# Block transposes on VectorE in place of TensorE's transposes for the modulation vector of the attention heads

## The reference, cut to what matters

```python
c_act = jax.nn.silu(c)                           # (1, 1024)
for i in range(DEPTH_2):
    mod = c_act @ w_ada[i] + b_ada[i]            # (1, 6 * 1024)
    sh1, sc1, g1, sh2, sc2, g2 = jnp.split(mod, 6, axis=-1)
...
shf, scf = jnp.split(c_act @ w_ada_final + b_ada_final, 2, axis=-1)
```

## Time and profile before

| | |
|---|---|
| median of 3 runs | 1554.79 us (1554.63 to 1555.78) |
| the profiled execution's own time | 1554.12 us |
| its span, first to last instruction | 1552.0 us |
| around the span | 2.12 us |
| instructions | 21277 |
| TensorE busy | 1537.0 us, 99% |
| VectorE / ScalarE / GpSimd busy | 790.5 / 597.4 / 869.6 us |
| mean granted TensorE clock | 0.998 |

### The profile page before, as it was taken

The page is one execution under the profiler, slowest core; times in us unless marked ns, Lnnn a source line. Parts: engine busy times, 40 slices in busy tenths (PEclk is TensorE's granted clock), DMA queues, the critical chain, the costliest instruction groups (busy, mean ns, idle before and its releaser), DMA issues.

```text
span 1552.0 us, 21277 instructions
## 1 busy us (share of the span) xinstructions
PE 1537.0 (99%) x7254; PEld 1273.8 (82%) x7254; DVE 790.5 (51%) x1128; ACT 597.4 (38%) x885; POOL 869.6 (56%) x1040
## 2 busy tenths in 40 slices
PE   9999999999999999999999999999999999999997
PEld 7777878887988888888888888888889888888886
DVE  6887776878645543551545424446257454011113
ACT  7444434685522212223444334244345322122223
POOL 6445538647567765775463635535535766555551
PEclk9999999999999999999999999999999999999999
DMA  6534455226265555542232322313212563223321
GB/s 231 191 128 155 164 214 189 82 84 205 95 216 176 202 198 183 192 160 95 89 114 67 109 82 80 97 52 106 95 54 82 201 206 120 98 95 95 95 82 55
DMA packets 58249, 202.97 MB, mean 131 GB/s; under 512 B 6480, under 2 KB 8528, under 8 KB 58192
## 3 DMA queue, kind: packets, MB, share of 16 engines
q1 hardware_dynamic: 56752, 198.74, 37.6%
q10 hardware_dynamic: 1440, 3.44, 0.7%
HBM read 200.05 MB, written 2.10 MB: 130 GB/s over the span
## 4 chain that ended last, share of the span: by engine, by line
PE 76%; POOL 12%; issue 11%; DVE 0%; DMA 0%; ACT 0%; SPq 0%; POOLq 0%; DVEq 0%; ACTq 0%
PE banks L1708 20%; PE banks L1712 20%; PE banks L1711 20%; POOL w_lo L411 12%; PE banks L2212 2%; PE banks L2211 2%; PE banks L2208 2%; PE banks L1724 1%; PE banks L1727 1%; PE banks L1728 1%; PE banks L2248 1%; PE banks L2247 1%; PE banks L2246 1%; PE banks L2235 0%; PE banks L2234 0%
## 5 line engine op out<-in xcount | busy, mean ns | idle before, releaser
L411 POOL TENSOR_TENSOR w_lo<-w_raw,w_hi 128x256 fp32r<-128x256 f32 x1028 | 862.6, 872 | 646.9 <-ACT w_hi L443 646.9
L443 ACT ACTIVATE w_hi<-w_raw 128x1024 fp32r<-128x1024 f32 x257 | 270.1, 1057 | 640.7 <-PE banks L1708 576.0
L1708 PE MATMUL banks<-a_hi,w_lo 128*128 128x512 f32 x1228 | 483.4, 394 | 0.2 <-POOL w_lo L411 0.2
L1712 PE MATMUL banks<-a_hi,w_hi 128*128 128x512 f32 x1228 | 478.2, 389 | 0.0
L1711 PE MATMUL banks<-a_lo,w_hi 128*128 128x512 f32 x1228 | 478.0, 389 | 0.0
L1708 PEld LDWEIGHTS banks<-a_hi,w_lo 128*128 128x128 f32 x1228 | 230.8, 188 | 49.0 <-issue 1.6
L1712 PEld LDWEIGHTS banks<-a_hi,w_hi 128*128 128x128 f32 x1228 | 230.5, 188 | 48.3
L1711 PEld LDWEIGHTS banks<-a_lo,w_hi 128*128 128x128 f32 x1228 | 230.6, 188 | 47.6 <-issue 1.0
L1708 PE MATMUL banks<-b_hi,w_lo 128*128 128x512 f32 x572 | 224.2, 392 | 2.3 <-POOL w_lo L411 2.1
L1712 PE MATMUL banks<-b_hi,w_hi 128*128 128x512 f32 x572 | 222.6, 389 | 0.0
L1711 PE MATMUL banks<-b_lo,w_hi 128*128 128x512 f32 x572 | 222.6, 389 | 0.0
(11 more groups left out here) (287 smaller groups left out, 1632.7 us busy)
## 6 DMA issues: line engine op xcount, KB each, us to landing
w_raw<-in_W SPq DMA_DIRECT2D x258, 512.0 KB, 3.5
ada_raw<-in_ADA SPq DMA_DIRECT2D x112, 512.0 KB, 4.3
X<-in_XT SPq DMA_DIRECT2D x8, 256.0 KB, 6.4
scr<-in_DECAY ACTq DMA_DIRECT2D x4, 448.0 KB, 4.0
out<-X SPq DMA_DIRECT2D x2, 512.0 KB, 3.0
w_raw<-in_W SPq DMA_DIRECT2D x2, 256.0 KB, 3.8
scr<-in_PT ACTq DMA_DIRECT2D x1, 512.0 KB, 4.8
scr<-in_ROPE ACTq DMA_DIRECT2D x1, 512.0 KB, 4.6
```

The lines of the kernel that those rows point to most:

```text
L411: pool.tensor_tensor(w_lo[:, c % RING, part], w_raw[:, c % RING, part], w_hi[:, c % RING, part].bitcast(fp32), ALU.subtract).then_inc(wlo, 1)
L443: act.activation(w_hi[:, c % RING, :], w_raw[:, c % RING, :], ACT.Copy).then_inc(whi, 1)
L1708: mm = pe.matmul(out, lo, x_hi, start=first, stop=False)
L1712: mm = pe.matmul(out, hi, x_hi, start=False, stop=last)
```

## The change

`ada_turn`, with its eight TensorE transposes a head at n = 17, goes. So does the branch of `ada_out` with two reductions from PSUM. In place of them VectorE transposes `ada_acc` in 32 x 32 blocks into `tmp` and sums it after L1285, TensorE makes four small products at n = 23, and `ada_out` adds the bias from `aux`. The folding matrix is made once ahead of the heads by three additions on VectorE.

```diff
+        head_turned = tmp[:, :, :].rearrange("p a s -> p (a s)")
+        head_fold, head_part = scr[:, 14 * S + 64:14 * S + 96], scr[:, 14 * S + 96:14 * S + 128]
...
-            def ada_out(u, g, at=flat, bank=None):
+            def ada_out(u, g, at=flat):
...
-                if bank is None:
-                    dve.tensor_tensor(dst, aux[:, 0:KD], b, ALU.add).then_inc(aux_free, 1)
-                    return
-                for n, half in enumerate((bank, 7)):
-                    turned = banks[:, half, :].rearrange("p (f q) -> p f q", q=P)
-                    ins = dve.tensor_reduce(ada_col[:, 4 * n:4 * n + 4], turned, AX.X, ALU.add)
-                link(ins, at)
-                dve.tensor_tensor(dst, ada_col, b, ALU.add).then_inc(aux_free, 1)
+                dve.tensor_tensor(dst, aux[:, 0:KD], b, ALU.add).then_inc(aux_free, 1)
...
+            def head_ada_fold(at):
+
+                dve.wait_ge(ada_sum, at("ada", KD))
+                dve.wait_ge(mix_ready, at("two", 2))
+                link(dve.transpose(head_turned, ada_acc[:, :]), at)
+                ins = dve.tensor_reduce(head_part, head_turned.rearrange("p (j q) -> p j q", q=32), AX.X, ALU.add)
+                ins.then_inc(head_folded, 1)
...
             link(dve.memset(G[:, 0:2], 0.0))
+            link(dve.tensor_tensor(head_fold, ident[:, 0:32], ident[:, 32:64], ALU.add))
+            for n in (2, 3):
+                link(dve.tensor_tensor(head_fold, head_fold, ident[:, 32 * n:32 * n + 32], ALU.add))
             dve.wait_ge(r_ready, 1)
...
-                ada_out(A0 + 6, 0, at, 4)
+                head_ada_fold(at)
+                ada_out(A0 + 6, 0, at)
...
-            def ada_turn(at, u, g, bank):
-
-                pe.wait_ge(ada_sum, at("ada", KD * (g + 1)))
+            def head_ada_rows(at, u):
+
+                pe.wait_ge(head_folded, at("one", 1))
                 pe.wait_ge(aux_free, at("aux", u))
-                for f in range(KD):
-                    out = banks[:, bank if f < KD // 2 else 7, f % 4 * P:(f % 4 + 1) * P]
-                    mm = pe.transpose(out, ada_acc[:, f * P:(f + 1) * P], ident)
+                for b in range(4):
+                    mm = pe.matmul(aux[32 * b:32 * b + 32, 0:KD], head_fold, head_part[:, b:32:4], start=True, stop=True)
                 mm.then_inc(aux_ready, 1)
...
-                if n == 17:
-                    ada_turn(at, A0 + 6, 0, 4)
+                if n == 23:
+                    head_ada_rows(at, A0 + 6)
```

More of the change, by code:

```diff
@@ L236, in build @@
         ada_in = [sem(f"ada_in{s}") for s in range(ADA_RING)]
-        ada_sum, ada_folded = sem("ada_sum"), sem("ada_folded")
+        ada_sum, ada_folded, head_folded = sem("ada_sum"), sem("ada_folded"), sem("head_folded")
         x_in = [sem(f"x_in{m}") for m in range(KD)]
```

## The result

The changed kernel takes 1561.3 us, median of 6 runs (1560.6 to 1564.97), against 1555.04 of 6 for the kernel before: ratio 1.0044, 95% interval 1.0033 to 1.0054 (the ratios are as recorded and differ by up to 0.0005 from the quotients of the medians, here 1.0040). It is slower, as forecast, but by 6.3 us, half as much again as the 4.2 that I had, and outside the range (1557.2 to 1560.6). Its profiled execution took 1564.64, with a span of 1562.7 against 1552.0.

A forecast was written before the change was run, and what follows sets the result against it. TensorE, busy 1537.0 of 1552.0 us, was taken to bound the kernel. Three heads lose 1.41, 1.38 and 1.38, in sum 4.17: 1554.12 + 4.17 = 1558.3, and the median 0.67 higher, 1559.0; range 1557.2 to 1560.6.

The forecast's parts named there:

- the mechanism and its sign: Head ends: `ada_out` waits for the small products ahead of two evacuations, which TensorE awaits; three heads slower, 4.17 us.
- the two prices on TensorE: In each head, eight transposes cost 0.88 us and four small products 0.38, so TensorE alone saves 0.50.
- the fourth head: Last head, no next one: its 0.50 us gain goes into a longer wait for `w_lo`, counted 0.
- the clock: Rival: TensorE's clock falls in the new 2.0 us standstills, 9.3 us more, 1568; chance 3%.
- the whole span's mean of 0.998 is a loss of 3.1 us at the start: Whole span: mean clock read as a 3.1 us loss at the start, used to price a fall after each standstill.
- the longest wait now is 1.33 us and the clock is 1.00 after it: TensorE before the change: full clock after its longest wait, 1.33 us, set against a fall in new waits of 2.0.
- the slack of the fold: Before the small products: VectorE's fold is ready 0.1 to 0.3 us early in the first head, 0.4 in the second.
- One small term: Signal from the fold's end on VectorE to TensorE's small products: some 0.05 us.
- a late fold: Rival: block transpose beside GpSimd and ScalarE takes 0.5 us more, TensorE waits, up to 1.5 more, 1560.5; chance 10%.
- whatever it sheds is gained: Inside the heads TensorE never waits, busy in all of 52.6 us, so all work removed from it is saved time.

The follow-up runs named there:

- pad_again: Changed kernel with eight unread 128x512 TensorE products between the small products and the wait for the next head's query and key, run beside the changed kernel: 1559.23 us, 1.0025.
- no_out: Changed kernel without `ada_out` for the heads, so their modulation vectors stay zero and VectorE goes straight from the fold to the evacuations: 1554.42 us, ratio 0.9998.
- fold_early20: Changed kernel with the fold moved ahead of L1285, into VectorE's wait for ScalarE's rounding, and the small products at tile 20: 1553.62 us, ratio 0.9989.
- behind25: Changed kernel with the next head's query and key evacuated before the fold and `ada_out`, and the small products at tile 25: 1553.24 us, ratio 0.9988.
- Experiment 5: ScalarE rounds two weight chunks between starting and awaiting the load of `p`: on the kernel before 1553.88 us, on `behind25` 1552.35 us.
- after_again: The changed kernel run again, unedited, on the same chip as the filled one: 1562.48 us, ratio 1.0044.
- pad: Changed kernel with eight unread 128x512 TensorE products between the small products and the wait for the next head's query and key, first time: 1560.38 us, ratio 1.0038.
- one_turn: The kernel before with one of the eight TensorE transposes a head kept, seven blocks not transposed: 1555.28 us, ratio 0.9998.
- before_p: The kernel before, with ScalarE rounding two weight chunks between starting the load of `p` and waiting for it: 1553.88 us, ratio 0.9991.

## Why the prediction was right and wrong

**Right: the mechanism and its sign.** `ada_out` ahead of the two evacuations exposes the trip to TensorE and back. Forecast 2.29 us from the products to the scores, measured 2.35 to 2.39; forecast 1.41 and 1.38 a head, measured 1.47 where the clock stays up (`pad_again`). Three ways of taking the trip out from between the fold and the scores (`no_out`, `fold_early20`, `behind25`) bring the time back to before or below. It is shown.

**Right: the two prices on TensorE.** 0.88 for the transposes less 0.38 for the products is 0.50 a head; `behind25` has 0.47 and 0.49, and its scores come 10.51 us behind the statistics in place of 11.41, so 0.90 for the transposes alone. The Trainium skill, "TensorE: Matmul & The Clock Gate", section "Part 4: PE-mode transpose", gives about 275 ns for a 128 x 128 transpose in a kernel. By an estimate from it, eight one after another, such a head would take 50.7 us; the trace disagrees, 52.07.

**Right, with luck in the size: the fourth head.** Its 0.50 was worth nothing in the profiled execution: the wait behind the load of `p` grew from 0.73 to 1.29 (timeline of TensorE after the change), where I had some 1.2. Experiment 5 shows the cause. But the same wait is 0.6, 1.0 and 1.3 in `after_again`, `pad_again` and `pad`, so one execution doesn't fix it.

```profile
251.13 0.47 PE L1715 MATMUL banks<-b_hi,w_lo 128*128 128x512 f32 x1 [1.29 <-POOL w_lo L413]
```

**Wrong: the clock. This is the step that failed.** The sum has no term for it. The forecast gave the fall 3%, as a rival, and put it against a reading that was false: "the whole span's mean of 0.998 is a loss of 3.1 us at the start". It isn't at the start, where the first 10 us have 1.00. The stretch of before that has it is the end, when TensorE is done:

```profile
1545.00:1552.00 7.00, 0.00 (x0) 0.00 (x0) 2.91 (x8) 2.91 (x8) 0.00 (x0) 0.51 0.75 254
```

And "the longest wait now is 1.33 us and the clock is 1.00 after it" was no ground to hold 2.0 to 2.1 safe; it bounds from one side alone. The falls cost 4.5 of the profiled execution's 10.7 us. In the runs of one chip, side by side, filling the standstills saved 3.2 (1562.48 against 1559.23). All eleven runs of the changed kernel have a mean clock of 0.995 to 0.997, all nine of `pad_again` 0.998 or more. `pad_again` is 4.4 us over before, where I had 4.17 for the whole change, and its 1559.23 lies inside my range. The first `pad`, with 5 runs, is 5.5 over.

**Wrong: the slack of the fold.** "The fold is ready by 0.1 to 0.3 us" was read from one execution in which the slabs landed well. Counted in the timelines from TensorE's output statistics (L1865) to the last slab's accumulation (L948), that one starts 3.13 to 3.43 us later in the four heads before, but 2.91 to 4.37 in the changed kernel's and 3.24 to 4.69 in `one_turn`. The change doesn't bring it: `before_p`, whose heads are those of the kernel before, has 3.59 to 4.15, and in its first head even that kernel waits for the evacuations (TensorE's timeline):

```profile
77.39 0.49 PE L1993 MATMUL banks<-scr 64*128 64x128 f32 x4 [0.32 <-DVE scr L1210]
```

One small term was mis-sized as well: 0.13 from the fold's end to TensorE (75.58 + 1.22 to 76.93), where I had 0.05. With it, and with the 0.11 from L1291's end to the block transpose, the first head's fold is ready at 72.82 + 0.11 + 2.50 + 0.13 = 75.56, against TensorE's 75.62, so nothing was to spare. For a late fold I had a rival (10%, up to 1.5) but took its cause from the engine beside it and not from the DMA wait, which stands in brackets in VectorE's rows. The sum had nothing for it; it cost 1.3 in the profiled execution.

**Wrong: "whatever it sheds is gained".** TensorE had no wait in the heads, but VectorE's evacuations ended only 0.5 us ahead of the scores in the first head and 0.75 in the other two. That, and not 0.88, is what could be shed there without turning VectorE's order, and less with a late slab; `one_turn` shows it.

**Open.** What decides in which head the clock falls: waits of 2.10 and 2.15 left it alone, 2.11 and 2.14 did not. In the changed kernel's heads the first fall has 0.83 of waiting right before it, but the second has none. Nor was it tried how the slabs' landing could be made steadier. And one run of the first `pad` took 1562.38 with a mean clock of 0.998, as high as before; there is no trace of it, and late slabs, which would fit, are not shown for it.

## What to carry to other kernels

A result fetched from another engine costs the whole trip, if what the other engine wants next stands behind the fetch on an in-order queue; put the work that it waits for first, and the fetch where an idle time lies. An engine that is busy for all of a stretch can still be within tenths of a microsecond of waiting for a neighbour, so read when each of its inputs was ready, in more than one head, before counting a saving. A new standstill of two microseconds on TensorE has a second price, the products at half speed behind it, so fill it or price it.

## What the runs showed of the hardware that was not expected

- TensorE's clock fell to the 1.2 GHz level behind standstills of 2.1 us in two of three heads, in two executions, for 6.9 and 3.5 us in the first of them, and behind one of 2.7 us in a third kernel. With eight otherwise useless products in the gap the two profiled executions (`pad`, `pad_again`) have no fall in the heads.
- VectorE's loop end takes 0.30 to 0.37 us where the turn ends with the short `ada_out` (0.17 us), behind a wait or not. Where it ends with a reduction of 1.22 us, the next turn's first instruction follows at once.
